# A recurrence beside projections: the second query unit is computed in front of the levels, twelve units stand beside them, rotations come two items earlier

## What is computed

```
def hgrn2_scan(q, k, v, logf):          # chunks of the sequence, 4 heads of 64
    b = cumsum(logf)
    o_inter = (q * exp(b)) @ state
    attn[t, s] = sum_k q[t] k[s] exp(b[t] - b[s])      (s <= t)
    o = o_inter + attn @ v
def mixer_b(q, f_fwd, f_bwd, i, g, ...):
    o_f = hgrn2_scan(q, 1 - f_fwd, i, log f_fwd)
    o_b = flip(hgrn2_scan(flip(q), flip(1 - f_bwd), flip(i), flip(log f_bwd)))
    return rms_norm(o_f + o_b, g_norm) * silu(g)
```

## Time and profile before

| | |
|---|---|
| median of 3 runs | 3247.87 us (3244.62 to 3250.11) |
| the profiled execution | 3245.03 us, span 3243.1 us |
| mean granted TensorE clock | 0.981 |
| PE busy | 3082.0 us, 95% of the span |
| DVE, ACT, POOL busy | 48%, 37%, 33% |
| chain that ended last | PE 82%, DVE 6%, POOL 4%, ACT 4% |

### The profile page before, as it was taken

One profiled execution on the slowest core, in us unless ns is written; L12 is line 12 of the kernel. 1 busy time (PEld: TensorE's weight loads), 2 busy tenths in 40 slices (PEclk: granted clock), 3 DMA queues, 4 the chain that ended last, 5 costly groups with the idle time before them and its releaser, 6 DMA issues.

```text
span 3243.1 us, 44526 instructions
## 1 busy us (share of the span) xinstructions
PE 3082.0 (95%) x18057; PEld 2473.3 (76%) x18057; DVE 1563.8 (48%) x1910; ACT 1191.8 (37%) x1917; POOL 1056.1 (33%) x503
## 2 busy tenths in 40 slices
PE   8989999999999989999999899989999899989999
PEld 6767688888887767787877677768877677778887
DVE  4354446462232466623312765477752875454420
ACT  3255422211223345423233435544332434544432
POOL 1302033323342311044453221235544321235553
PEclk9999999999999999999999999999999999999999
DMA  6101024342221133344332212046654222023332
GB/s 211 43 6 40 1 72 137 95 120 65 59 59 52 40 97 94 92 111 111 99 90 75 70 46 68 29 131 190 184 170 128 67 53 68 21 77 96 96 96 91
DMA packets 442375, 279.73 MB, mean 86 GB/s; under 512 B 113610, under 2 KB 419516, under 8 KB 441788
## 3 DMA queue, kind: packets, MB, share of 16 engines
q1 hardware_dynamic: 442172, 276.87, 29.9%
HBM read 274.73 MB, written 2.10 MB: 85 GB/s over the span
## 4 chain that ended last, share of the span: by engine, by line
PE 82%; DVE 6%; POOL 4%; ACT 4%; issue 3%; DMA 1%; SPq 0%; DVEq 0%; ACTq 0%; POOLq 0%
PE ps L660 55%; PE ps L1265 4%; POOL WL L2200 3%; PE ps L1087 3%; PE ps L1097 2%; PE ps L1341 2%; PE ps L1114 1%; PE ps L1363 1%; PE ps L1334 1%; PE ps L1155 1%; PE ps L1145 1%; ACT WH L1632 1%; PE ps L1172 1%; PE ps L1405 1%; PE ps L818 1%
## 5 line engine op out<-in xcount | busy, mean ns | idle before, releaser
L2200 POOL TENSOR_TENSOR WL<-RAW,WH 128x1024 fp32r<-128x1024 f32 (+2 forms) x364 | 877.4, 2411 | 1837.3 <-ACT WH L1632 1828.1
L660 PE MATMUL ps<-HH,WH 128*128 128x512 f32 (+1 forms) x2184 | 728.3, 371 | 31.4 <-POOL WL L2200 24.1
L660 PE MATMUL ps<-HH,WL 128*128 128x512 f32 (+1 forms) x2184 | 720.5, 367 | 0.0
L660 PE MATMUL ps<-HL,WH 128*128 128x512 f32 (+1 forms) x2184 | 719.9, 367 | 0.0
L1632 ACT ACTIVATE WH<-RAW 128x1024 fp32r<-128x1024 f32 (+2 forms) x364 | 377.0, 1036 | 409.7 <-PE ps L660 280.9
L660 PEld LDWEIGHTS ps<-HH,WH 128*128 128x128 f32 x2184 | 377.1, 189 | 116.1 <-POOL WL L2200 32.4
L660 PEld LDWEIGHTS ps<-HH,WL 128*128 128x128 f32 x2184 | 376.5, 189 | 69.6
L660 PEld LDWEIGHTS ps<-HL,WH 128*128 128x128 f32 x2184 | 375.6, 189 | 68.4 <-issue 0.7
L660 PE MATMUL ps<-FH,WH 128*128 128x512 f32 x352 | 138.1, 392 | 4.9 <-POOL WL L2200 4.7
L2452 DVE SCALAR_TENSOR_TENSOR XT<-RAW,CS,XT 128x1024 f32<-128x1024 f32 x77 | 130.3, 1693 | 20.2 <-DMA RAW<-in_w_ada 18.9
L660 PE MATMUL ps<-FH,WL 128*128 128x512 f32 x352 | 137.2, 390 | 0.0
(11 more groups left out here) (420 smaller groups left out, 5230.0 us busy)
## 6 DMA issues: line engine op xcount, KB each, us to landing
RAW<-in_w_in SPq DMA_DIRECT2D x122, 512.0 KB, 3.8
RAW<-in_w_ada SPq DMA_DIRECT2D x96, 512.0 KB, 3.8
RAW<-in_w_up SPq DMA_DIRECT2D x88, 512.0 KB, 4.6
RAW<-in_w_in SPq DMA_DIRECT2D x72, 256.0 KB, 3.6
RAW<-in_w_mod SPq DMA_DIRECT2D x32, 512.0 KB, 3.6
RAW<-in_w_down SPq DMA_DIRECT2D x32, 512.0 KB, 3.8
WMOD<-in_w_mod SPq DMA_DIRECT2D x8, 1024.0 KB, 13.9
RAW<-in_w_branch SPq DMA_DIRECT2D x16, 512.0 KB, 3.4
```

The lines of the kernel that those rows point to most:

```text
L660: ins = nc.tensor.matmul(ps[0:width, t0:t0 + tn], a, b[:, k0 + k, t0:t0 + tn], start=first and k == 0 and i == 0, stop=last and k == kt - ...
L2200: nc.gpsimd.tensor_tensor(WL[s % NWS][:, 0:used], RAW[n % NRAW][:, 0:used], WH[s % NWS][:, 0:used].bitcast(F32), ALU.subtract).then_inc(*u ...
```

## The change

The second query unit ("bq", 1) moves from the units beside the levels to those in front of them. Twelve units are left beside the levels, two halves each, for 24 items; before, the thirteenth, ("cq", 3), was computed after item 23 and the spreads. From the second unit on each unit beside the levels, and what is turned with it, comes two items earlier. On VectorE the four rotation steps move from items 12, 14, 16, 18 to 10, 12, 14, 16. The loads on SP and the splits on ScalarE and GpSimd follow the order of the units; GpSimd's clears of DIAG stand at the same places in `BESIDE`, the first two after one split more.

```diff
-        FIRST_UNITS = [("bff", 0), ("bfb", 0), ("bff", 1), ("bfb", 1), ("bg", 0), ("bg", 1), ("bq", 0)]
-        BESIDE = [("bi0ch", 0), ("bq", 1), ("bi1ch", 0), ("avch", 0), ("aq", 0), ("aq", 1), ("aq", 2), ("aq", 3),
+        FIRST_UNITS = [("bff", 0), ("bfb", 0), ("bff", 1), ("bfb", 1), ("bg", 0), ("bg", 1), ("bq", 0), ("bq", 1)]
+        BESIDE = [("bi0ch", 0), ("bi1ch", 0), ("avch", 0), ("aq", 0), ("aq", 1), ("aq", 2), ("aq", 3),
                   ("cvch", 0), ("cq", 0), ("cq", 1), ("cq", 2), ("cq", 3)]
...
-                    if s in (2 * SPAN, 2 * SPAN + 2, 2 * SPAN + 4, 2 * SPAN + 6):
-                        turn2(l, (s - 2 * SPAN) // 2)
+                    if s in (2 * SPAN - 2, 2 * SPAN, 2 * SPAN + 2, 2 * SPAN + 4):
+                        turn2(l, (s - 2 * SPAN + 2) // 2)
```

## The result

The changed kernel takes 3267.24 us (median of 4 runs, 3263.41 to 3270.06) against 3246.24 us for the kernel before beside it; the ratio is 1.0062, with 1.005 to 1.0074 as its 95% interval. It is slower by about 21 us, and the forecast was 3266.6. Runs of one kernel scatter by 5 to 17 us, so the segments of the traces are a better measure of the mechanism than the medians.

A forecast was written before the change was run, and what follows sets the result against it. TensorE, busy 95% of the span, was taken to bound the kernel. Per layer +5.5, +0.9, +3.0 and 0, then -1.5 or 0 and +0.7, gave 8.6 and 10.1, together +18.7: 3266.6 us, range 3254 to 3279.

The forecast's parts named there:

- Step 1: In front of item 0: one more unit delays item 0 by 5.5 us per layer, the 4.5 us idle stays.
- Steps 2 and 3: Levels, per layer: sums of (cq,2) before CBIAS's issue, +0.9 us; new PSUM slot neighbours make TensorE wait, +3.0 us.
- The upper bound: Levels: +6.4 us for the PSUM slot waits if each of the two long new ones also drops the clock.
- Step 4: Levels: rotations two items earlier on VectorE cost 0, or +0.7 us if its chain were late.
- Step 5: CBIAS issue to attention: TensorE idles 6 to 8 us for w_out's second unit; -1.5 and 0, plus 0.7 low clock.
- S: End of the levels: the moment SP issues CBIAS, after the last value group; predicted 9.4 us later per layer.
- Fewer new waits: Rival, levels: PSUM slots free themselves in time, -0.6 in place of 3.0 us; total 3259.4 us, chance 0.11.
- more clock falls: Rival, levels: stops at items 10 and 17 drop the clock, VectorE late at item 11; +5 us, 3271.6, chance 0.12.
- An early landing: Rival, attention start: w_out's weights land with CBIAS, 9.3 us after its issue; total 3259.5 us, chance 0.05.
- A filled front: Rival, before item 0: ScalarE's exponentials don't wait, idle and low clock go; -13.4 us, 3253.2, chance 0.06.
- a fast end: Attention start follows TensorE, 11.3 us after CBIAS's issue, 4.1 and 6.5 us less; part of a 0.06 rival.
- "faster" rival: Front and attention start: ScalarE's order holds up TensorE at neither; -6.7 us in all, 3241.2 us, chance 0.06.

The follow-up runs named there:

- e1: Changed kernel, but ScalarE makes the exponentials of items 0 and 1 before waiting for and copying unit (bq,1): 3252.88 us, 1.0019 times the kernel before.
- e3: Changed kernel, but SP sends CBIAS one unit later, so w_out's second unit is sent before it: 3253.84 us, 1.0015 times the kernel before.
- e7: Changed kernel, DMAs unmoved, but ScalarE and GpSimd split w_out's second unit later, at the attention's sixth pair: 3255.82 us, 1.0029 times the kernel before.
- e8: The changed kernel repeated as it is: 3265.63 us, 1.0058 times the kernel before.
- e2: Changed kernel, but a hand-written table gives each recurrence group's PSUM slot: 3251.86 us, 1.001 times the kernel before.

## Why the prediction was right

**Step 1, the front.** Summed at +5.5, measured +5.43 and +5.41. The idle time stayed at 4.55 and its chain is the same; e1 shows by removal that it was the wait for (bq,1) and its copy, ahead of the exponentials.

**Steps 2 and 3, the levels.** Summed at +0.9 and +3.0, measured +4.34 and +2.80, in the mean 3.6. The wait list grew by 2.8, each new wait at the group and behind the copy that the count by hand named: 0.78 where 0.85 was taken, 1.36 twice, 0.54 less for weights at item 10, 0.10 less at lev 16. The two layers differ by the low clock behind the stop: the first half unit takes 4.74 us in layer 0 (4.10 before) and 3.95 in layer 1 (4.64 before). That I had carried as equal. The low clock behind the stop was short in layer 1 of this execution alone: e3, e7 and e8, which leave this stretch as it is, need 135.1 to 135.7 us for it in both layers, 3.9 to 4.5 more than the kernel before. The upper bound, a clock fall at the new waits, did not come.

**Step 4, rotations.** Taken at 0. In the changed kernel the cross items wait for nothing, so it held. e2 shows how thin this was: with the slot waits gone the cross group of item 11 waits 0.26 us for KX, behind `turn2(0)` and `keep_level(9)` in VectorE's queue, and that of item 17 waits 0.96, behind `turn2(3)` and `keep_level(15)`.

**Step 5, the end.** The mechanism held: ScalarE waits 11.3 and 12.2 us for the second w_out unit ("some 10"). The idle came out at 4.9 and 8.0 in place of "6 to 8". TensorE was done at S+11.5 in layer 0, where "about S+9.5" was taken, since the clock fell while it still made its sums (0.64 from 1990 to 1993 us, then 0.50); in layer 1 it was done at S+9.4. This costs nothing while the transfer ends last. Sizes: I gave -1.5 and 0 and measured -0.45 and -0.38. In layer 0 the last transfer took 9.3 us and not 8.2, so it landed 12.7 us after the issue instead of 11.6; in layer 1 it came 0.4 earlier. The low clock afterwards cost 0.35 and 1.16 up to w_out where 0.7 each was taken.

**Sum.** 8.6 and 10.1 forecast, 9.67 and 8.99 in the trace; 18.7 both times. That the totals agree to the tenth is luck. The levels came out 0.7 us under their sum and the end 0.7 over it, both layers together. And the trace of the same kernel in e8, cut at the same marks, gives 11.8 and 11.3 us more than the kernel before, 23.1 together: 1.6 of that is a low clock in front of the stop in layer 0, and its end is later than before by 0.3 in each layer, not earlier. So the sum is right to some 4 us, not to a tenth.

**The rivals.** Fewer new waits and more clock falls: neither in the trace. An early landing: in no run did the second w_out unit land within 9.3 us of CBIAS's issue when it stood behind it; it took 12.7 and 13.6 us here and up to 14.5 in e1. The 358 GB/s of the Trainium skill, page "DMA: Bandwidth & Descriptors", section "Where 436 GB/s comes from", from which 9.2 us had been estimated, don't fit this trace: CBIAS came at up to 445 GB/s, what stood behind it at 211 to 226. A filled front and a fast end are what e1 and e3 had to make by hand; the deciding points named for them, the exponentials close behind the distances and the weights landed early, are just what those edits set. The sum of the "faster" rival has a slip: its terms give S+10.3 and not S+11.3, so 3239.2 in place of 3241.2. e3 measured 10.8 and 12.0.

## What to carry to other kernels

Moving work into an idle stretch of the bound engine fills it only if no other engine's queue has the next step behind that work's result: look at which instruction will wait for the moved product, and what stands behind it. Work that trails a stage may cover a transfer that the wait list hardly names (in the kernel before ScalarE waits 1.7 us for it in one layer and not at all in the other); before it is moved away, read what the next stage's first instruction stands behind. With buffers taken in turn, one group more or less changes who follows whom, so count the slots through before and after, and let no group follow a unit that has just ended.

## What the runs showed of the hardware

In layer 1 the clock stays low longer after the longer stop than I had taken. Windows across the start of the attention in layer 1 of the changed kernel (us; busy of PE, PEld, DVE, ACT, POOL; PEclk; DMA share; GB/s):

```profile
2734.00:2737.00 3.00, 3.00 (x26) 2.40 (x22) 1.29 (x2) 0.00 (x0) 0.00 (x0) 1.00 1.06 445
2737.00:2740.00 3.00, 1.50 (x8) 0.65 (x8) 0.00 (x0) 0.00 (x0) 0.00 (x0) 0.73 1.03 211
2740.00:2743.00 3.00, 0.00 (x0) 0.00 (x0) 0.00 (x0) 0.24 (x1) 0.00 (x0) 0.50 1.22 226
...
2749.00:2752.00 3.00, 3.00 (x18) 1.45 (x14) 1.61 (x3) 0.66 (x3) 0.00 (x0) 0.50 0.38 109
2752.00:2755.00 3.00, 3.00 (x42) 2.58 (x40) 1.89 (x3) 2.47 (x6) 1.27 (x1) 0.99 0.01 3
```

TensorE takes up at 2746.48 and has 1.2 GHz (0.50) for about 5.5 us more. Before, it took up at 2723.23 and had it for 2.9. The 2.6 us more at half speed would cost 1.3 by estimate, and transposes to w_out took 1.16 us longer. In layer 0 the low clock lasted 4.1 us in place of 3.1 and the cost was 0.35.

The DMA columns show two rates of one queue: 445 GB/s while CBIAS comes in whole rows of 21504 bytes, 211 to 226 while w_out's pieces of 512 bytes do, with the DMA engines busy all the time (DMA share 1.03 and 1.22). From 2737 us to the landing at 2742.7 some 1.2 MB of these pieces come, more than twice the 512 KB of the second unit: transfers of the unit after it, issued from 2733.2 on, run beside its last one, and three of them land before it. By estimate the 512 KB alone would take 2.4 us at this rate in place of 5.7; no run has them alone behind CBIAS.
